# Hybrid decoder layer on one core: first norms, held-back sums and transfers moved in the paired projections

## The chip, the core and the metric

The kernel runs on one core of one Trainium2 chip. A core has five engines that run side by side: TensorE (PE in the profile; its weight loads are PEld) for matmuls, VectorE (DVE), ScalarE (ACT), GpSimd (POOL) and SyncE (SP), which here only issues DMAs. Each engine works through its own list of instructions in order. The engines wait for each other by semaphores. The metric is the time of one execution in device microseconds (us); lower is better.

## What is computed

One decoder layer on a sequence of 1024 tokens of width 1024, in float32:

```python
h = modulate(rms_norm(x), shift1, scale1)
proj = h @ w_in                      # 1024 x 3600, split into nine parts
# group A: 4 heads of gated linear attention (pairs P0, P1 in the kernel)
# group B: 4 heads of HGRN2 (H0, H1, H1, H1), forget = lb + (1-lb)*sigmoid(hf)
def chunk_gated_linear_attention(q, k, v, log_a, chunk=64):
    cum = cumsum(log_a within the chunk)
    q_rel, k_rel = q * exp(cum - cum_mid), k * exp(cum_mid - cum)
    scores = where(causal, q_rel @ k_rel.T, 0);  o_intra = scores @ v
    chunk_update = (k * exp(cum_last - cum)).T @ v
    state = exp(cum_last) * state + chunk_update      # scan over 16 chunks
    return o_intra + (q * exp(cum)) @ state_before
o = rms_norm(o, gain) * silu(gate)   # for each head, then concatenated
x = x + gate1 * (concat(o) @ w_out)
h = modulate(rms_norm(x), shift2, scale2)
x = x + gate2 * (square(relu(h @ w_mlp1)) @ w_mlp2)
return rms_norm(x, final_norm_g)
```

## The kernel before

Every matmul with weights is done in a split form. A float32 operand is written as a high part in the format fp32r and a low part, and a product is three matmuls: high times high, low times high, high times low. ACT copies the high part of a weight tile (`pw_hi`, `w_hi`, `wr_hi`), and POOL or DVE subtracts to get the low part (`pw_lo`, `w_lo`, `wr_lo`).

The stages follow each other on PE: transposes of x and norms; the groups P0, P1 and H0, in which each column block of `w_in` is a plain product with 2 x 8 x 3 matmuls; then, from about 225 us on, four "paired" groups (three H1 and the last, G); then the output projection (about 440 to 533 us) and the MLP.

In a paired group two pairs of column blocks are computed, the early one (p even) and the late one (p odd), eight pairs in all (p = 0 to 7). A pair is a 2 x 2 block product done by Strassen's scheme with seven smaller products: six (`pair_product`, P1 to P6, twelve 128x512 matmuls each, 4 tiles by 3) and a seventh, P7, which is cut in four pieces (`seventh_piece`, three matmuls each), whose input operand comes from HBM (`t3_scratch`, tiles `piece_x` for pieces 0 and 2, `piece_y` for 1 and 3). The sums of weight quarters that the scheme needs (`weight_sum_of`, kinds S1 to S4) and the sums of the results (`join`) are done by DVE. `copy_part` on ACT keeps a partial result. The sums of inputs for P5 and P4 (`t1`, `t4`, from `x_sum`) are made once, by DVE and ACT, before and in pair 0.

Between these products PE does the attention of the head before, in steps `attend(n)`: transposes (`k_end`, `vT`), chunk updates (`v_nat`, `k_nat`), scores (`q_rel`, `k_rel`), outputs (`masked`, `state`) and the sums of squares for the norm of a head ("ss", matmuls with `ones` on `sq_hi` and `sq_lo`). For the norm, ACT does a logarithm and an exponential (`norm_log`, `norm_exp`, in H0 inside `read_out`), each behind a load of another activation table, and DVE multiplies (`norms`).

The order on each engine is the order in which the code is written: nothing is scheduled by a planner. What an engine does late, all that stands behind it does late too. SP's list of DMAs is such a list as well: a `wait_ge` in it holds all later transfers back.

The names that matter below: on DVE, `group` ends H0, with `weight_sum_of(0, "S2")`, the sum and difference of `x_sum` (`add_parts`, `subtract`), the first norms (`read_out(7)`) and the gate; `paired` is a paired group (L2703 on). On ACT, `group` and `paired`; on PE, `two_pairs`; on SP, `load_piece`, `load_pair_quarter`, `load_out`, `load_x_back`.

## Time and profile before

| | us |
|---|---|
| median of 3 runs (lowest, highest) | 1165.41 (1165.19, 1165.82) |
| the profiled execution | 1166.44 |
| its span, first to last instruction | 1164.7 |
| PE busy | 1137.4 (98%) |
| DVE busy | 876.3 (75%) |
| ACT busy | 612.9 (53%) |
| POOL busy | 499.4 (43%) |
| mean granted clock of TensorE, share of full | 0.993 |

The busy time of PE counts each matmul from its start to its modelled end, and the next one starts before that end. So a gap on PE that is shorter than about 0.16 us doesn't show as idle, and one that shows is 0.16 us longer when counted from start to start. The times of the other engines are those of their instructions, waiting inside an instruction included. The DMA queues moved 180.44 MB, 155 GB/s on average.

### The profile page before, as it was taken

What the parts mean: (1) busy time and instruction counts of PE and PEld (TensorE: products, weight loads), DVE (VectorE), ACT (ScalarE), POOL (GpSimd) and SP (SyncE); (2) the same over time, 40 slices, a digit from 0 to 9 for tenths busy, and PEclk for the clock granted to TensorE, in tenths of its full rate; (3) what the DMA queues carried; (4) which work ended last, traced back from release to release, by engine and by line L of the source; (5) the groups of instructions that cost most, each with busy time, mean ns of one, the idle gap of its engine ahead of it and who ended that gap; (6) DMA issues with size and microseconds to landing.
All of it is one profiled execution on the core that took longest, in us unless ns stands there. A gap on an engine that the chain in (4) does not pass through costs nothing.

```text
span 1164.7 us, 15675 instructions
## 1 busy us (share of the span) xinstructions
PE 1137.4 (98%) x5555; PEld 939.3 (81%) x5555; DVE 876.3 (75%) x1048; ACT 612.9 (53%) x933; POOL 499.4 (43%) x318
## 2 busy tenths in 40 slices
PE   7999999899999999999999999999999999999996
PEld 6788788787878787888888888888888888788885
DVE  6898888877777677477976765677795884966776
ACT  7763564756566566345654555455664433424424
POOL 1021111534243344427534353344466675666741
PEclk9999999999999999999999999999999999999999
DMA  9777353044353549421455344544624637447203
GB/s 359 259 235 271 128 175 97 1 127 129 93 177 98 154 123 295 143 93 73 137 170 181 136 155 135 181 144 157 194 64 159 223 91 264 147 132 279 72 1 145
DMA packets 160549, 180.44 MB, mean 155 GB/s; under 512 B 7508, under 2 KB 119256, under 8 KB 157784
## 3 DMA queue, kind: packets, MB, share of 16 engines
q1 hardware_dynamic: 160472, 179.44, 46.4%
q8 instruction: 45, 0.74, 0.3%
q14 instruction: 32, 0.26, 0.1%
HBM read 138.51 MB, written 40.89 MB: 154 GB/s over the span
## 4 chain that ended last, share of the span: by engine, by line
PE 89%; DVE 4%; DMA 2%; ACT 2%; issue 1%; SPq 1%; POOL 1%; DVEq 0%; ACTq 0%
PE unit_bank L1742 16%; PE unit_bank L2156 9%; PE unit_bank L2158 9%; PE unit_bank L2157 9%; PE small_bank L2156 9%; PE small_bank L2158 9%; PE small_bank L2157 9%; PE unit_bank L2003 3%; PE small_bank L1742 3%; PE unit_bank L2005 3%; PE unit_bank L2004 3%; PE small_bank L1879 2%; DVE ada_acc L2257 1%; PE small_bank L1781 1%; DMA ada_slot<-in_w_ada_dram 1%
## 5 line engine op out<-in xcount | busy, mean ns | idle before, releaser
L997 POOL TENSOR_TENSOR wr_lo<-quarter,wr_hi 128x512 fp32r<-128x512 f32 x122 | 197.6, 1632 | 174.4 <-ACT wr_hi L1530 174.3
L2156 PE MATMUL unit_bank<-op_hi,wr_hi 128*128 128x512 f32 x452 | 176.5, 390 | 1.1 <-issue 1.1
L2158 PE MATMUL unit_bank<-op_hi,wr_lo 128*128 128x512 f32 x452 | 175.9, 389 | 0.0
L2157 PE MATMUL unit_bank<-op_lo,wr_hi 128*128 128x512 f32 x452 | 175.9, 389 | 0.0
L2156 PE MATMUL small_bank<-op_hi,wr_hi 128*128 128x512 f32 x448 | 174.5, 390 | 0.0
L2158 PE MATMUL small_bank<-op_hi,wr_lo 128*128 128x512 f32 x448 | 174.3, 389 | 0.0
L2157 PE MATMUL small_bank<-op_lo,wr_hi 128*128 128x512 f32 x448 | 174.3, 389 | 0.0
L1530 ACT ACTIVATE wr_hi<-wr_full 128x512 fp32r<-128x512 f32 x90 | 56.8, 631 | 173.3 <-DVE wr_full L2903 173.3
L2903 DVE TENSOR_TENSOR wr_full<-quarter,quarter 128x512 f32<-128x512 f32 x90 | 88.9, 989 | 56.3 <-PE small_bank L2158 23.0
L1530 ACT ACTIVATE wr_hi<-quarter 128x512 fp32r<-128x512 f32 x136 | 83.0, 626 | 90.5 <-PE unit_bank L2158 48.4
L1742 PE MATMUL unit_bank<-a_hi,w_hi 128*128 128x512 f32 x304 | 121.2, 399 | 0.8 <-DVE w_lo L2401 0.8
L1742 PE MATMUL unit_bank<-a_lo,w_hi 128*128 128x512 f32 x304 | 118.5, 390 | 0.0
L1742 PE MATMUL unit_bank<-a_hi,w_lo 128*128 128x512 f32 x304 | 118.4, 390 | 0.0
L997 POOL TENSOR_TENSOR wr_lo<-wr_full,wr_hi 128x512 fp32r<-128x512 f32 x48 | 80.2, 1673 | 77.0 <-ACT wr_hi L1530 65.6
L2156 PEld LDWEIGHTS unit_bank<-op_hi,wr_hi 128*128 128x128 f32 x452 | 84.8, 188 | 19.5 <-issue 2.1
L2157 PEld LDWEIGHTS unit_bank<-op_lo,wr_hi 128*128 128x128 f32 x452 | 84.9, 188 | 17.8 <-issue 0.2
L2158 PEld LDWEIGHTS unit_bank<-op_hi,wr_lo 128*128 128x128 f32 x452 | 84.8, 188 | 17.7
L2158 PEld LDWEIGHTS small_bank<-op_hi,wr_lo 128*128 128x128 f32 x448 | 84.1, 188 | 17.6
L2156 PEld LDWEIGHTS small_bank<-op_hi,wr_hi 128*128 128x128 f32 x448 | 84.1, 188 | 17.4 <-POOL wr_lo L997 0.2
L2157 PEld LDWEIGHTS small_bank<-op_lo,wr_hi 128*128 128x128 f32 x448 | 84.1, 188 | 17.4
L930 POOL TENSOR_TENSOR w_lo<-raw,w_hi 128x1024 fp32r<-128x1024 f32 x11 | 28.8, 2614 | 150.8 <-ACT w_hi L1054 150.8
L972 POOL TENSOR_TENSOR pw_lo<-pw_full,pw_hi 128x512 fp32r<-128x512 f32 x24 | 39.7, 1654 | 85.7 <-ACT pw_hi L1315 68.9
(366 smaller groups left out, 2397.2 us busy)
## 6 DMA issues: line engine op xcount, KB each, us to landing
quarter<-in_w_mlp_dram SPq DMA_DIRECT2D x128, 256.0 KB, 4.1
hidden_scratch<-hid SPq DMA_DIRECT2D x98, 256.0 KB, 2.4
ada_slot<-in_w_ada_dram SPq DMA_DIRECT2D x48, 512.0 KB, 6.1
op_full<-hidden_scratch SPq DMA_DIRECT2D x21, 1024.0 KB, 4.8
pair_quarter<-in_w_in_dram SPq DMA_DIRECT2D x32, 256.0 KB, 3.7
piece_x<-t_scratch SPq DMA_DIRECT2D x16, 512.0 KB, 4.1
piece_y<-t_scratch SPq DMA_DIRECT2D x32, 256.0 KB, 3.3
raw<-in_w_out_dram SPq DMA_DIRECT2D x16, 512.0 KB, 4.5
```

Source lines behind the costliest of these rows:

```text
L930: pool.tensor_tensor(w_lo[slot][:, :, :], raw[slot][:, :, :], w_hi[slot][:, :, :].bitcast(F32), ALU.subtract).then_inc(wlo_ready, 1)
L972: pool.tensor_tensor(pw_lo[place][:, :, :], pair_source(prod), pw_hi[place][:, :, :].bitcast(F32), ALU.subtract).then_inc(pair_lo, 1)
L997: pool.tensor_tensor(wr_lo[slot][:, :, :], split_source(n), wr_hi[slot][:, :, :].bitcast(F32), ALU.subtract).then_inc(wr_lo_pool, 1)
L1530: act.activation(wr_hi[slot][:, :, :], split_source(n), ACT.Copy).then_inc(wr_hi_ready, 1)
L1742: return pe.matmul(out_ap, left, right, start=start, stop=stop)
L2003: pe.matmul(dst, wh, hi[:, k, :], start=k == 0 and prod not in (P6, P3), stop=False, skip_group_check=True)
L2004: pe.matmul(dst, wh, lo[:, k, :], start=False, stop=False, skip_group_check=True)
L2005: mm = pe.matmul(dst, wl, hi[:, k, :], start=False, stop=k == KH - 1, skip_group_check=True)
L2156: pe.matmul(dst, wh, ah, start=opens, stop=False, skip_group_check=True)
L2157: pe.matmul(dst, wh, al, start=False, stop=False, skip_group_check=True)
L2158: mm = pe.matmul(dst, wl, ah, start=False, stop=k == KH - 1, skip_group_check=True)
L2903: dve.tensor_tensor(dst[:, :, :], a[:, :, :], b[:, :, :], op).then_inc(w_sum, 1)
```

## The change

The diff moves work; the arithmetic is the same. By part:

1. SP: a `piece_x` transfer of 512 KB becomes two of 256 KB. The copies of x back from HBM (`xT`, 4 x 1 MB) are no longer issued in one go ahead of the third weight tile of the output projection but one at a time between the weight tiles, and the eight first MLP quarters are issued after the eighth weight tile, not after the fourth.
2. ACT, end of H0: the two logarithms of the first norms stay, then come the copy of the keys and of the partial result and the high part of P6, then the two exponentials, the high part of P5 and the high part of `t4`.
3. DVE, same place: S2 of pair 0 is done before `decay` and `q_cum`; the sums of inputs for `t4` wait until the low part of P2 of pair 0 is made; S1 and the first join stand before the norms; the gate stands behind `t4_lo`.
4. PE, pair 0: pieces 1 and 2 of P7 stand behind P5, piece 3 behind P4. In all pairs: `attend(5)`, the first sum of squares, stands in the middle of P1 of the late pair.
5. All paired groups: ACT makes `sq_hi` before it copies the output; DVE does S4 and the second `sq_lo` of the late pair right after the first join, before `decay`, `q_cum` and `q_rel`; ACT does the high part of the next P7 before the second norm's logarithm and exponential, and the last value copy right behind them.

```diff
@@ SP
-                if j % 2:
-                    for i in range(2):
-                        sp.dma_start(piece_y[i][:, :].bitcast(F32), t3_dram[:, j, i, :]).then_inc(piece_y_loaded, 16)
-                else:
-                    sp.dma_start(piece_x[120 if p < 5 else 96][:, :, :].bitcast(F32), t3_dram[:, j]).then_inc(piece_x_loaded, 16)
+                for i, part in enumerate(piece_place(p, j)):
+                    sp.dma_start(part.bitcast(F32), t3_dram[:, j, i, :]).then_inc(piece_y_loaded if j % 2 else piece_x_loaded, 16)
...
-            for i in range(2):
-                load_x_back(i)
-            for v in range(2, 4):
+            load_x_back(0, 0)
+            load_out(2)
+            load_x_back(1, 0)
+            for v in range(3, OUT_HALVES):
                 load_out(v)
-            sp.wait_ge(normed, before("ss", 7))
...
+                if v in (5, 6):
+                    load_x_back(v - 5, 1)
+                if v == 7:
+                    sp.wait_ge(normed, before("ss", 7))
...
@@ ACT
-                    read_out(7, "ss")
-                    act.wait_ge(t_done, T_DONE_0 + 1)
...
-                    act.activation(tok(mixed[:, gi + 1], half), src, ACT.Copy).then_inc(read["o"], 1)
                     act.wait_ge(o_squared, before("o", gi) + half + 1)
                     act.activation(sq_hi[:, 0, :], stat[:, 0, :], ACT.Copy).then_inc(sq_hi_ready, 1)
+                    act.activation(tok(mixed[:, gi + 1], half), src, ACT.Copy).then_inc(read["o"], 1)
...
+                    first_logs()
+                    keys(0)
+                    copy_part(early, 0)
+                    pair_high(early, P6)
+                    first_exps()
+                    pair_high(early, P5)
+                    fourth_high()
                 pair_high(early, P4)
...
+                pair_high(late + 1, P7)
                 norm_log(1)
                 norm_exp(1)
-                pair_high(late + 1, P7)
+                value_of(0, late, "21")
                 pair_high(late + 1, P2)
-                value_of(0, late, "21")
@@ PE
+                    if between and k == 1:
+                        between()
...
                 pair_product(early, P6)
+                if early:
+                    seventh_piece(early, 2)
+                attend(2)
+                pair_product(early, P5)
                 if not early:
                     seventh_piece(early, 1)
-                seventh_piece(early, 2)
-                attend(2)
-                pair_product(early, P5)
-                seventh_piece(early, 3)
+                    seventh_piece(early, 2)
+                else:
+                    seventh_piece(early, 3)
                 attend(3)
                 pair_product(early, P4)
+                if not early:
+                    seventh_piece(early, 3)
                 attend(4)
                 pair_product(early, P3)
-                attend(5)
-                pair_product(late, P1)
+                pair_product(late, P1, lambda: attend(5))
@@ DVE
                 read_out(6)
+                if own == "H":
+                    weight_sum_of(0, "S2")
...
-                    weight_sum_of(0, "S2")
+                    dve.wait_ge(pair_lo, PAIR_LO_0 + split_of(0, P2))
                     add_parts(xs[2], 1, 0, 7)
                     subtract(xs[2], xs[2], xs[3], 8)
-                read_out(7)
+                if own == "P":
+                    read_out(7)
...
-                if own == "H":
-                    gate(u0 + 3, hh, hh)
...
                 join(early, "11")
+                if early == 0:
+                    first_norms()
                 states(0)
                 if early == 0:
                     low_fourth()
+                    first_gate()
...
                 join(late, "11")
+                weight_sum_of(late, "S4")
+                low_squares(1)
                 dve.wait_ge(read["up"], before("chunks", gi + 1))
...
-                weight_sum_of(late, "S4")
-                low_squares(1)
                 join(late, "u")
```

`first_logs`, `first_exps`, `first_norms`, `first_gate` and `fourth_high` hold the instructions that `read_out(7, "ss")`, `read_out(7)` and `gate` held before, with the same shapes.

DVE at the border of H0 and pair 0, before. `pair_quarter_186` is S2, `pw_full_201` S1, `pw_full_198` S4, `x_sum_204` the sum of inputs for `t4`, `unit_bank<-unit_bank,k_end` the first join, `COPY_PREDICATED` the mask of the first scores.

```order
L2584 COPY decay<-cum 128x16
L2587 SCALAR_TENSOR_TENSOR q_cum<-t_177,cum 128x1024
L2619 TENSOR_TENSOR pair_quarter_186<-pair_quarter_189,pw_full_199 128x512
L2408 TENSOR_TENSOR x_sum_204<-a_hi,a_lo 128x2048
L2414 TENSOR_TENSOR x_sum_204<-x_sum_204,x_sum_205 128x2048
L2493 SCALAR_TENSOR_TENSOR mixed<-mixed,cols,stat 128x512 x2
L2510 SCALAR_TENSOR_TENSOR t_177<-t_177,t_178 128x1024
L2515 SCALAR_TENSOR_TENSOR mixed<-t_177,mixed 128x1024
L2619 TENSOR_TENSOR pw_full_201<-pair_quarter_188,pair_quarter_189 128x512
L2646 TENSOR_TENSOR unit_bank<-unit_bank,k_end 128x512
L2679 SCALAR_TENSOR_TENSOR state<-state,decay,small_bank 128x128 x8
L2430 TENSOR_TENSOR t_lo<-x_sum_204,t_hi 128x2048
L2619 TENSOR_TENSOR pw_full_198<-pair_quarter_187,pair_quarter_186 128x512
```

And now:

```order
L2651 TENSOR_TENSOR pair_quarter_186<-pair_quarter_189,pw_full_199 128x512
L2600 COPY decay<-cum 128x16
L2603 SCALAR_TENSOR_TENSOR q_cum<-t_177,cum 128x1024
L2435 TENSOR_TENSOR x_sum_204<-a_hi,a_lo 128x2048
L2441 TENSOR_TENSOR x_sum_204<-x_sum_204,x_sum_205 128x2048
L2651 TENSOR_TENSOR pw_full_201<-pair_quarter_188,pair_quarter_189 128x512
L2678 TENSOR_TENSOR unit_bank<-unit_bank,k_end 128x512
L2621 SCALAR_TENSOR_TENSOR mixed<-mixed,cols,stat 128x512 x2
L2711 SCALAR_TENSOR_TENSOR state<-state,decay,small_bank 128x128 x8
L2457 TENSOR_TENSOR t_lo<-x_sum_204,t_hi 128x2048
L2628 SCALAR_TENSOR_TENSOR t_177<-t_177,t_178 128x1024
L2631 SCALAR_TENSOR_TENSOR mixed<-t_177,mixed 128x1024
L2651 TENSOR_TENSOR pw_full_198<-pair_quarter_187,pair_quarter_186 128x512
```

S2 went ahead of `decay`, S1 and the join ahead of the norms, and the two rows of the gate from before S1 to before S4.

PE in pair 0, before: the last matmuls of P6, pieces 1 and 2, the first scores, then P5 (`t_hi`).

```order
L2003 MATMUL unit_bank<-a_hi,pw_hi_190 128x512
L2004 MATMUL unit_bank<-a_lo,pw_hi_190 128x512
L2005 MATMUL unit_bank<-a_hi,pw_lo_194 128x512
L2023 MATMUL unit_bank<-piece_y_214,pw_hi_191 128x512
L2024 MATMUL unit_bank<-piece_y_215,pw_hi_191 128x512
L2025 MATMUL unit_bank<-piece_y_214,pw_lo_195 128x512
L2023 MATMUL unit_bank<-piece_x_212,pw_hi_191 128x512
L2024 MATMUL unit_bank<-piece_x_212,pw_hi_191 128x512
L2025 MATMUL unit_bank<-piece_x_212,pw_lo_195 128x512
L1742 MATMUL small_bank<-q_rel,k_rel 128x128 x4
L2003 MATMUL unit_bank<-t_hi,pw_hi_193 128x512
```

And now, behind P5: pieces 1 and 2, then the transposes of the second keys and the second scores, then P4.

```order
L2026 MATMUL unit_bank<-t_hi,pw_lo_197 128x512
L2046 MATMUL unit_bank<-piece_y_214,pw_hi_191 128x512
L2047 MATMUL unit_bank<-piece_y_215,pw_hi_191 128x512
L2048 MATMUL unit_bank<-piece_y_214,pw_lo_195 128x512
L2046 MATMUL unit_bank<-piece_x_212,pw_hi_191 128x512
L2047 MATMUL unit_bank<-piece_x_212,pw_hi_191 128x512
L2048 MATMUL unit_bank<-piece_x_212,pw_lo_195 128x512
L1802 MATMUL small_bank<-ident,k_end 128x128 x4
L1763 MATMUL small_bank<-q_rel,k_rel 128x128 x4
L2024 MATMUL unit_bank<-t_hi,pw_hi_192 128x512
```

The two pieces went behind the first scores and P5, so the second scores follow them closely; piece 3, which stood ahead of the key transposes, is now behind P4.

DVE in the late pair of a paired group (here p = 1), before: the first join, `decay`, `q_cum` (in `cum`), `q_rel`, S4 (`pw_full_198`), `sq_lo`, the second join.

```order
L2646 TENSOR_TENSOR unit_bank<-unit_bank,k_nat 128x512
L2755 COPY decay<-cum 128x16
L2760 SCALAR_TENSOR_TENSOR cum<-q_rel,cum 128x1024
L2763 SCALAR_TENSOR_TENSOR q_rel<-q_rel,t_177 128x1024
L2619 TENSOR_TENSOR pw_full_198<-pair_quarter_187,pair_quarter_186 128x512
L2686 TENSOR_TENSOR sq_lo<-stat,sq_hi 128x512
L2646 TENSOR_TENSOR t_178<-unit_bank,k_nat 128x512
```

And now:

```order
L2678 TENSOR_TENSOR unit_bank<-unit_bank,k_nat 128x512
L2651 TENSOR_TENSOR pw_full_198<-pair_quarter_187,pair_quarter_186 128x512
L2718 TENSOR_TENSOR sq_lo<-stat,sq_hi 128x512
L2792 COPY decay<-cum 128x16
L2797 SCALAR_TENSOR_TENSOR cum<-q_rel,cum 128x1024
L2800 SCALAR_TENSOR_TENSOR q_rel<-q_rel,t_177 128x1024
L2678 TENSOR_TENSOR t_178<-unit_bank,k_nat 128x512
```

S4 and `sq_lo` passed the three instructions that make `decay`, `q_cum` and `q_rel`.

## Rows read from the trace of the kernel before

**Rows 1.** The page, part 1: busy us (share of the span) and instructions.

```profile
PE 1137.4 (98%) x5555; PEld 939.3 (81%) x5555; DVE 876.3 (75%) x1048; ACT 612.9 (53%) x933; POOL 499.4 (43%) x318
```

**Rows 2.** Waits of PE, whole span: engine, line, waited for: us in total, times, longest.

```profile
PE small_bank L1742 <- DVE sq_lo L2686: 3.8, 6, 0.9
PE unit_bank L2003 <- POOL pw_lo L972: 1.9, 1, 1.9
...
PE unit_bank L2023 <- POOL pw_lo L972: 0.8, 1, 0.8
PE unit_bank L1742 <- DVE w_lo L2401: 0.8, 1, 0.8
PE small_bank L1781 <- ACT vT L1378: 0.3, 1, 0.3
```

**Rows 3.** Busy time by stretch: length, busy of PE, PEld, DVE, ACT, POOL, PEclk, DMA.

```profile
500.00:600.00 100.00, 100.00 (x439) 82.10 (x438) 86.72 (x86) 55.61 (x83) 49.83 (x32) 1.00 0.32 107
231.50:238.00 6.50, 6.02 (x18) 4.41 (x20) 5.61 (x6) 4.67 (x8) 2.49 (x2) 0.50 0.45 130
```

**Rows 4.** Timeline of PE, pair 0: start, us, instruction, count [idle before, releaser].

```profile
228.71 0.50 PE L2023 MATMUL unit_bank<-piece_x,pw_hi 128*128 128x512 f32 x1 [0.81 <-POOL pw_lo L972]
...
231.98 0.80 PE L2003 MATMUL unit_bank<-a_hi,pw_hi 128*128 128x512 f32 x1 [1.87 <-POOL pw_lo L972]
...
247.78 1.06 PE L1742 MATMUL small_bank<-q_rel,k_rel 128*128 128x128 f32 x8
...
254.01 0.48 PE L2003 MATMUL unit_bank<-a_hi,pw_hi 128*128 128x512 f32 x1
```

**Rows 5.** Timeline of POOL, pair 0 (us of each instruction).

```profile
225.40 3.26 POOL L972 TENSOR_TENSOR pw_lo<-pw_full,pw_hi 128x512 fp32r<-128x512 f32 x1 [2.73 <-DVE pair_quarter L2619]
228.62 3.31 POOL L972 TENSOR_TENSOR pw_lo<-pair_quarter,pw_hi 128x512 fp32r<-128x512 f32 x1
...
239.90 1.29 POOL L972 TENSOR_TENSOR pw_lo<-pair_quarter,pw_hi 128x512 fp32r<-128x512 f32 x1
```

**Rows 6.** Timeline of DVE, pair 0.

```profile
224.63 0.69 DVE L2619 TENSOR_TENSOR pair_quarter<-pair_quarter,pw_full 128x512 f32<-128x512 f32 x1
...
227.56 3.25 DVE L2414 TENSOR_TENSOR x_sum<-x_sum,x_sum 128x2048 f32<-128x2048 f32 x1
232.35 1.42 DVE L2493 SCALAR_TENSOR_TENSOR mixed<-mixed,cols,stat 128x512 f32<-128x512 f32 x2 [1.55 <-ACT stat L1234]
...
236.08 1.77 DVE L2619 TENSOR_TENSOR pw_full<-pair_quarter,pair_quarter 128x512 f32<-128x512 f32 x1
...
244.69 0.74 DVE L2666 COPY_PREDICATED masked<-causal,small_bank 128x512 f32<-128x512 uint32 x1
```

**Rows 7.** Timeline of ACT, pair 0.

```profile
230.40 1.28 ACT L1234 ACT_TABLE_LOAD   x1
231.69 1.15 ACT L1234 ACTIVATE stat<-stat 128x512 f32<-128x512 f32 x2
...
235.07 0.57 ACT L1329 ACTIVATE k_nat<-small_bank 128x512 f32<-128x512 f32 x1
```

**Rows 8.** Timelines of PE, DVE and ACT, end of pair 3 (late pair of the second paired group).

```profile
330.03 0.47 PE L1742 MATMUL small_bank<-sq_hi,ones 128*128 128x512 f32 x1 [0.95 <-DVE sq_lo L2686]
...
338.94 1.07 PE L1781 MATMUL small_bank<-ident,vT 128*128 128x128 f32 x8
...
325.07 2.27 DVE L2760 SCALAR_TENSOR_TENSOR q_cum<-q_rel,q_cum 128x1024 f32<-128x1024 f32 x1
...
332.51 0.68 DVE L2619 TENSOR_TENSOR pw_full<-pair_quarter,pair_quarter 128x512 f32<-128x512 f32 x1
...
338.22 0.58 ACT L1378 ACTIVATE vT<-unit_bank 128x512 f32<-128x512 f32 x1
```

**Rows 9.** Timelines of SP's queue and PE, first products of the output projection.

```profile
438.93 7.38 SPq L780 DMA_DIRECT2D raw<-in_w_out_dram  x2
...
452.46 0.50 PE L1742 MATMUL unit_bank<-a_hi,w_hi 128*128 128x512 f32 x1 [0.75 <-DVE w_lo L2401]
```

69 lines of the change are left out of this document (41 added, 28 removed).

## The prediction

> **What bounds the kernel now.** I read the page's shares first, then PE's waits, then busy time by stretch, then the timelines at each wait. The shares say that PE is busy 98% of the span, DVE 75%, ACT 53%, POOL 43% [rows 1]. PE runs the same 5555 matmuls after the change, so only its gaps and its clock can be won. The waits that the change aims at are few: six for the low part of the squares, 3.8 us, two for POOL's low parts, 1.9 and 0.8, one for the low part of an output weight, 0.8, and one for a value copy, 0.3 [rows 2]. Counted from start to start each is 0.16 longer, which makes about 4.8, 3.0, 0.9 and 0.5 us. One more loss is no wait: at 231.5 to 238.0 the granted clock is 0.50 of full, 1.2 GHz, and 18 matmuls took 6.02 us, against 439 in 100 us (0.228 each) at full clock [rows 3]. PE had just waited 0.81 at 228.71 and 1.87 at 231.98 [rows 4]. The 18 hold a few short ones, so I put the loss at 2.7 us rather than 6.02 - 18 x 0.228 = 1.9. All of it together is about 11.8 us, the most that can be won: 1165.4 - 11.8 = 1153.6.
>
> The sums below are made in the profiled execution, whose span is 1164.7 and whose own time is 1166.44, 1.03 above the median of 1165.41. The difference found there is taken off the median.
>
> **Output projection (part 1).** The third weight tile is issued at 438.93 and its transfer is followed by the wait of 0.75 for `w_lo` at 452.46 [rows 9], because 4 MB of `xT` stand ahead of it. Now 1 MB stands there. At the profile's mean of 155 GB/s 3 MB are some 19 us, at the rate of a busy stretch less, in each case far more than 0.75. The wait goes: -0.9. What was issued early is now late: the rest of `xT`, and 8 MLP quarters of 256 KB behind the eighth tile. They are needed at 533 us, after a stretch of 93 us in which PE is full; I cost them at 0, covered by that stretch, and at up to +1 if the last quarter is late for the first MLP product. Splitting `piece_x` in two costs SP another issue, 16 times, on a queue that runs ahead: 0.
>
> **End of H0 and pair 0 (parts 2 to 4).** Before, DVE does S2 at 224.63 and then, without a pause, the sum and the difference of `x_sum`; the difference took 3.25 against the 2.24 of the sum (from 225.32 to 227.56) [rows 6]. POOL's two low parts beside them took 3.26 and 3.31, and alone 1.29 [rows 5]. So the two engines exclude each other when both read two operands from SBUF, and each second one is 2 us late. Now S2 ends 0.9 earlier, at about 224.2, POOL starts earlier and alone, and P7's low part is there at about 226.5 and P2's at 227.8, instead of 228.66 and 231.93 [rows 5]. Both waits of [rows 4] and the low clock behind them go: 0.97 + 2.03 + 2.7 = 5.7.
>
> What is late next is DVE's own chain. The sums of inputs now wait for P2's low part, until 227.8; sum and difference then take 2 x 2.24, to 232.3, where before they ended at 227.56 + 3.25 = 230.81. From there to the first mask at 244.69 are 13.88 us, of which DVE waited 1.55 for the exponentials [rows 6], so 12.33 without that wait. The same instructions stand in that stretch after the change, in another order, with S1 (1.77) and a join first. (The 1.77 of S1 holds about 1.1 of standing behind POOL, against 0.69 for S2; POOL's low parts of P6 and P5 still lie beside this stretch, so I leave it in.) S1 and the join cover the wait: the exponentials, which come behind the key copy (0.57 [rows 7]), the high part of P6 and a load of 1.28, begin to land near 234.5 (the logarithms end at 230.4 plus the 0.65 that S2 puts ahead of `q_cum`, then 0.57 + 0.57 + 0.6 + 1.28 and half of 1.15). So the mask starts at 232.3 + 12.33 = 244.6, as before, and ends 0.74 later, at 245.35.
>
> The second scores go into the bank of the first and can't start before that. Before, PE reached them at 247.78 [rows 4], when the mask was long done. Now PE is there 5.7 earlier, less another 0.7 since piece 3 (three matmuls of 0.228) moved behind P4, plus a new wait: P6's high part is made behind the logarithms and the key copy, at about 232.6, and its low part, 1.29 later and behind the difference, at some 234.2, while PE comes to P6 at about 232.8. That is 1.4. So PE is at the second scores at 242.8 and waits 2.55. It goes on at 245.35 in place of 247.78 - 0.7: a lead of 1.7, and P3 starts at 252.3, not 254.01.
>
> Behind PE's second scores and `ss(0)` the next late thing is the turn to the next pair, where PE needs the value copy of ACT. That copy hangs on DVE's and ACT's chain (output, squares, norm, join, S3), which starts from a mask that is where it was. So of the lead of 1.7 most is returned there. I take -0.3 for the whole part; bounds: -1.7 if the chain has slack that I don't see, and +1.5 if it comes out later (the two waits that I add, 1.4 and 2.55, are to about 0.5 each).
>
> The Trainium skill, "ScalarE: Activation LUTs", section "What ACT_TABLE_LOAD costs", gives 1283 ns for the load and 1380 ns more of drain at each switch. The row has 1.28 at 230.40 and the exponential at 231.69, directly behind it [rows 7]: no second part shows after the load. By the page's price the exponentials would end 1.4 later, which is rival C; by the row they don't.
>
> **Late pairs (part 5, and `attend(5)` of part 4).** Before, PE waits for `sq_lo` twice a group, e.g. 0.95 at 330.03, since `sq_lo` stands behind `q_cum` (2.27) and more on DVE [rows 8]. With S4 and `sq_lo` ahead of them it is some 2 us earlier, and the wait goes; with the first `ss` in the middle of P1 the other goes as well. That is 1.6 a group, 4.8 in all. But the turn is tight already: the value copy runs 338.22 to 338.80 and PE's transposes start at 338.94 [rows 8]. It is ACT's, behind both table loads of the second norm, and these wait for S3 and the high and low parts of P7. On DVE, `q_cum` and `q_rel` are now some 1.4 later (S4 and `sq_lo` first), the second join 0.2 to 0.3 later, S3 at about 332.8 against 332.51. ACT wins something, because the high part of P7 and the logarithm are in a better order: I find the copy 0.3 earlier, at 337.95. So PE, ahead by 1.6, waits about 1.5 for it and keeps 0.3 a turn. There are three turns, of which the last two are sure: -0.6. Bounds: -4.8 if the copy moves with PE, +0.9 if it comes 0.3 later each time.
>
> **Sum.** -0.9 - 0.3 - 0.6 = -1.8: 1165.4 - 1.8 = 1163.6. From the bounds near it (part one -0.9 to 0, pair 0 -1 to +1, turns -1.5 to +0.9) the forecast's own range is 1162.2 to 1165.5.
>
> **Rivals.**
>
> A, the copy has slack: the waits for squares are truly saved and only pair 0 is given back. Then -0.9 - 0.3 - 4.8 = -6.0, 1159.4. For it: PE waited just 0.3 for a value copy in the whole span [rows 2], so it is a bottleneck once, not three times. Against it: 0.14 between the copy's end and PE's start at 338.94.
>
> A2, all is kept, pair 0 too: 1153.6. Against it: DVE's 12.33 us between difference and mask, which the change doesn't shorten.
>
> B, the other side: the new waits lower TensorE's clock. Before, 0.81 and 1.87 within 4 us put it at 0.50 for 6.5 us, at a cost of 2.7 [rows 3, 4]; single waits of 0.95 [rows 8] and 0.75 [rows 9] didn't. Now there are 1.4 at P6 and 2.55 at the second scores, and about 1.5 at three turns. In pair 0 a drop is paid from the lead. At the turns there is none: three drops would be 3 x 2.7 = 8.1, less the 1.8, or 1171.7; one or two of them 1166.3 to 1169.0. I take two, 1168 to 1169, as its time. It decides as soon as PE's wait at a turn, with what lies near it, weighs like the pair at 228.71 to 231.98.
>
> C, the exponentials are late. DVE comes to the norms at 232.3 + 1.77 + 0.7 = 234.8, only 0.3 behind their end by my count. If they end 1.4 later, the norms, the mask and all behind it come 1.1 later than before, and PE, which waits for that chain at the next turn, with them: -1.8 + 1.1 = -0.7, 1164.7. For it: ACT now does three operations more between the logarithms and the exponentials. Against it: the load of 1.28 has the exponential directly behind it [rows 7]. By the Trainium skill's price for a switch (same page and section) this is what would happen.
>
> D, the gain of part 1 is lost to a late MLP quarter (+1): 1164.6.
>
> **How the numbers follow.** Forecast 0.50 (in it that 0.02), A 0.27, A2 0.05, B 0.14, C and D 0.02 each. A measurement of this kernel tells 0.2%, 2.3 us, from no change. Faster than 1163.1 are A, A2 and about a fifth of the forecast: 0.42. Slower than 1167.7 is B, two drops or more, 0.12, and 0.02 for a turn that comes later than my bound. The rest, 0.44, is within. The range reaches over A to 1158.0 and on the other side to 1167.0, which leaves out A2 and most of B, 0.17.
>
> **What would show it.** Right: no wait for `w_lo` near 450; POOL's low parts of P7 and P2 in 1.3 each; DVE idle about 2.4 before the sum of inputs; the first mask at 244.6; PE waiting about 2.5 for it, and about 1.4 for P6's low part; the granted clock full around 231; waits for `sq_lo` under 0.5 in total beyond pair 0, and waits for the value copy up from 0.3 to 3 or 4 us. Wrong: a mask earlier than 243.5, a P3 of pair 0 and a turn both over 1 us earlier (A or A2), a clock of 0.50 behind a turn (B), norms on DVE after 235.5 (C), or a new wait at the start of the MLP (D).

## The result: slower by 0.6%

| | before | changed |
|---|---|---|
| median of 6 runs (lowest, highest) | 1166.41 us (1165.19, 1170.06) | 1174.27 us (1171.65, 1174.86) |
| span of the profiled execution | 1164.7 | 1172.1 |
| PE busy | 1137.4 | 1139.6 |

The ratio is 1.006, with a 95% interval of 1.0043 to 1.0077: slower, by 7 to 8 us, where 1.8 us less was forecast. The predicted range ended at 1167.0.

PE's waits in the profile of the changed kernel, which answer to [rows 2]; the columns are the same:

```profile
PE small_bank L1802 <- ACT vT L1391: 4.7, 3, 2.4
...
PE unit_bank L2046 <- POOL pw_lo L970: 2.3, 2, 1.2
PE unit_bank L2024 <- POOL pw_lo L970: 2.1, 3, 1.2
...
PE unit_bank L2024 <- DVE unit_bank L2678: 1.9, 3, 0.7
PE small_bank L1763 <- DVE masked L2698: 1.6, 1, 1.6
...
PE small_bank L1763 <- DVE sq_lo L2718: 1.0, 1, 1.0
```

The waits for `sq_lo` fell from 3.8 to 1.0 and those for `w_lo` are gone. In their place stand 4.7 for the value copy, 2.3 and 2.1 for POOL's low parts, 1.9 for a join, 1.6 for the mask. Where in the program this happens is best seen with PE's own landmarks: the first product of pair 0, the transposes of `vT` at the three turns from a paired group to the next, the first product with the third weight tile of the output projection, and the first product of the MLP. Both columns are differences of start times on PE's timeline.

| stretch of PE | before | changed | difference |
|---|---|---|---|
| to pair 0 | 224.91 | 224.72 | -0.19 |
| pair 0 to the first turn | 60.88 | 63.06 | +2.18 |
| first to second turn | 53.15 | 56.03 | +2.88 |
| second to third turn | 53.03 | 56.90 | +3.87 |
| third turn to the third weight tile | 60.49 | 60.50 | +0.01 |
| from there to the MLP | 77.25 | 77.07 | -0.18 |
| MLP to the end | 634.99 | 633.82 | -1.17 |
| sum, the span | 1164.7 | 1172.1 | +7.4 |

The loss is made between pair 0 and the third turn, +8.9 in all. PE's timeline there, changed kernel (start, us, instruction, idle before and its releaser):

```profile
234.00 0.50 PE L2024 MATMUL unit_bank<-a_hi,pw_hi 128*128 128x512 f32 x1 [1.21 <-POOL pw_lo L970]
...
241.89 0.50 PE L2046 MATMUL unit_bank<-piece_x,pw_hi 128*128 128x512 f32 x1 [0.55 <-DMA piece_x<-t_scratch]
...
244.83 2.08 PE L1763 MATMUL small_bank<-q_rel,k_rel 128*128 128x128 f32 x8 [1.55 <-DVE masked L2698]
...
287.78 1.06 PE L1802 MATMUL small_bank<-ident,vT 128*128 128x128 f32 x8 [1.13 <-ACT vT L1391]
290.00 0.47 PE L2046 MATMUL unit_bank<-piece_x,pw_hi 128*128 128x512 f32 x1 [1.15 <-POOL pw_lo L970]
...
335.65 0.47 PE L2024 MATMUL unit_bank<-a_hi,pw_hi 128*128 128x512 f32 x1 [0.65 <-DVE unit_bank L2678]
...
343.81 1.94 PE L1802 MATMUL small_bank<-ident,vT 128*128 128x128 f32 x8 [2.44 <-ACT vT L1391]
...
400.71 1.06 PE L1802 MATMUL small_bank<-ident,vT 128*128 128x128 f32 x8 [1.08 <-ACT vT L1391]
```

Pair 0 went as predicted up to the second scores: the two waits and the low clock at 231 are gone, PE waits 1.21 for P6's low part (1.4 forecast) and then, until 244.83, for the first mask, which DVE starts at 244.06 (244.6 forecast, 244.69 in [rows 6]). Of the two low parts that POOL now makes earlier, that of P2 took 1.29, as forecast, and that of P7 2.29, for 1.3 forecast. A wait of 0.55 for a `piece_x` transfer at 241.89 was not foreseen; it only shortens the wait for the mask. The turns did not go as predicted: at each PE waits 1.1 to 2.4 for the value copy, and the first piece of the next P7 starts 2.2 behind the transposes (at the first and third turn with a wait of 1.15 in between; at the second the transposes themselves are slow, 1.94 for 1.06). In the kernel before the piece started 1.18 behind them:

```profile
338.94 1.07 PE L1781 MATMUL small_bank<-ident,vT 128*128 128x128 f32 x8
340.12 0.47 PE L2023 MATMUL unit_bank<-piece_x,pw_hi 128*128 128x512 f32 x1
```

TensorE's granted clock falls at two places of this execution (busy time by stretch, columns as in [rows 3]):

```profile
245.00:250.00 5.00, 5.00 (x20) 4.39 (x21) 0.69 (x1) 0.99 (x2) 1.90 (x2) 0.71 0.72 229
345.00:350.00 5.00, 4.73 (x15) 3.58 (x14) 1.98 (x3) 3.21 (x7) 1.94 (x2) 0.50 0.22 65
```

At 345 to 350 that is the lower level, 1.2 GHz, throughout; at 245 to 250 it is a part at 1.2 and a part at 2.4 GHz. Now the chain that leads to the turn, on the engines that PE waits for. DVE of the changed kernel in the late pair ahead of the second turn:

```profile
326.83 0.69 DVE L2678 TENSOR_TENSOR unit_bank<-unit_bank,k_nat 128x512 f32<-128x512 f32 x1
327.43 1.19 DVE L2651 TENSOR_TENSOR pw_full<-pair_quarter,pair_quarter 128x512 f32<-128x512 f32 x1
328.58 1.73 DVE L2718 TENSOR_TENSOR sq_lo<-stat,sq_hi 128x512 fp32r<-128x512 f32 x1
330.24 1.26 DVE L2792 COPY decay<-q_cum 128x16 f32<-128x16 f32 x1
331.53 1.23 DVE L2797 SCALAR_TENSOR_TENSOR q_cum<-q_rel,q_cum 128x1024 f32<-128x1024 f32 x1
...
334.01 0.68 DVE L2678 TENSOR_TENSOR t<-unit_bank,k_nat 128x512 f32<-128x512 f32 x1
...
336.73 1.78 DVE L2651 TENSOR_TENSOR pw_full<-pair_quarter,pair_quarter 128x512 f32<-128x512 f32 x1
...
343.21 0.75 DVE L2725 SCALAR_TENSOR_TENSOR mixed<-mixed,cols,stat 128x512 f32<-128x512 f32 x1 [3.37 <-ACT stat L1363]
```

and POOL and ACT beside it:

```profile
328.02 1.75 POOL L970 TENSOR_TENSOR pw_lo<-pair_quarter,pw_hi 128x512 fp32r<-128x512 f32 x1
330.12 1.34 POOL L970 TENSOR_TENSOR pw_lo<-pw_full,pw_hi 128x512 fp32r<-128x512 f32 x1 [0.35 <-ACT pw_hi L1328]
336.45 1.51 POOL L970 TENSOR_TENSOR pw_lo<-pair_quarter,pw_hi 128x512 fp32r<-128x512 f32 x1 [4.98 <-ACT pw_hi L1328]
```

```profile
335.74 0.63 ACT L1328 ACTIVATE pw_hi<-pair_quarter 128x512 fp32r<-128x512 f32 x1 [1.01 <-DMA pair_quarter<-in_w_in_dram]
...
338.60 0.63 ACT L1328 ACTIVATE pw_hi<-pw_full 128x512 fp32r<-128x512 f32 x1 [1.74 <-DVE pw_full L2651]
339.25 1.28 ACT L1358 ACT_TABLE_LOAD   x1
...
341.26 1.28 ACT L1363 ACT_TABLE_LOAD   x1
342.55 0.63 ACT L1363 ACTIVATE stat<-stat 128x512 f32<-128x512 f32 x1
343.09 0.58 ACT L1391 ACTIVATE vT<-unit_bank 128x512 f32<-128x512 f32 x1
```

The same two joins and the end of the exponential in the kernel before:

```profile
323.77 0.69 DVE L2646 TENSOR_TENSOR unit_bank<-unit_bank,k_nat 128x512 f32<-128x512 f32 x1
...
329.80 0.68 DVE L2646 TENSOR_TENSOR t<-unit_bank,k_nat 128x512 f32<-128x512 f32 x1
```

```profile
336.64 0.63 ACT L1350 ACTIVATE stat<-stat 128x512 f32<-128x512 f32 x1
```

From join to join DVE took 6.03 us before and takes 7.18 now (326.83 to 334.01): S4, `sq_lo` and the small `decay` copy cost 1.19, 1.73 and 1.26, because POOL's low parts at 328.02 and 330.12 lie beside them. Start to start these three take 4.10, and took 1.90 before, where S4 and `sq_lo` needed 0.68 each. `q_cum` is quicker for it (1.23, [rows 8] has 2.27). Then S3 takes 1.78 beside POOL's 336.45, where it took 0.68 [rows 8]. From the join's start to the end of the exponential it was 7.47 us before (329.80 to 337.27) and is 9.17 now (334.01 to 343.18), because ACT's high part of P7 (338.60) waits for that S3 and the logarithm with its table load stands behind it. Together that is 1.15 + 1.70 = 2.85. From the end of the exponential to the first piece of P7 it is 2.85 in both kernels, and from that piece to the next first join 36.8 in both (36.80 and 36.83). So the 1.15 and the 1.70 are the whole loss of this period, counted from piece to piece: 53.15 before, 56.02 now (that the leg behind the exponential is 2.85 long as well is a coincidence). The value copy does come sooner behind the exponential (PE's transposes start 0.63 behind its end, before 1.67), but that wins nothing, because PE then stands at the piece.

The third period is made up otherwise. S3 took 0.69 at the third turn, so join to exponential is 8.08, 0.6 over the old 7.47; join to join is 7.18 again; and from the piece to the first join it is 38.80, 2.0 more than at full clock, in the stretch that begins with the low clock.

### The profile page after: what moved, and what is told of

Its sections match the earlier page's. It is cut to its first block, busy times and chain, and to the rows that moved or that the text cites. A ratio compares the mean times of both kernels' runs of the same rounds, so it can differ in the third digit from the quotient of the medians.

```text
span 1172.1 us, 15691 instructions
## 1 busy us (share of the span) xinstructions
PE 1139.6 (97%) x5555; PEld 940.7 (80%) x5555; DVE 877.7 (75%) x1048; ACT 612.9 (52%) x933; POOL 497.7 (42%) x318
## 4 chain that ended last, share of the span: by engine, by line
PE 82%; DVE 6%; ACT 4%; issue 3%; DMA 2%; POOL 1%; SPq 1%; DVEq 0%; ACTq 0%
PE unit_bank L1763 17%; PE unit_bank L2183 9%; PE unit_bank L2185 9%; PE unit_bank L2184 9%; PE small_bank L2185 9%; PE small_bank L2183 9%; PE small_bank L2184 9%; PE small_bank L1763 3%; PE unit_bank L2024 2%; PE unit_bank L2025 2%; PE unit_bank L2026 2%; DVE ada_acc L2284 1%; PE small_bank L1900 1%; PE small_bank L1802 1%; DMA ada_slot<-in_w_ada_dram 1%
## 5 line engine op out<-in xcount | busy, mean ns | idle before, releaser
L970 POOL TENSOR_TENSOR pw_lo<-pair_quarter,pw_hi 128x512 fp32r<-128x512 f32 x32 | 45.1, 1412 | 70.2 <-ACT pw_hi L1328 70.2
```

Source lines behind the costliest of these rows:

```text
L970: pool.tensor_tensor(pw_lo[place][:, :, :], pair_source(prod), pw_hi[place][:, :, :].bitcast(F32), ALU.subtract).then_inc(pair_lo, 1)
```

## The experiments

The landmarks of all kernels, in the same stretches; "ratio" is to the kernel before, of runs on the same chip, with its 95% interval.

| kernel | pair 0 to turn 1 | turn 1 to 2 | turn 2 to 3 | ratio |
|---|---|---|---|---|
| before | 60.88 | 53.15 | 53.03 | 1 |
| changed | 63.06 | 56.03 | 56.90 | 1.006 (1.0043 to 1.0077) |
| e1, late pairs undone | 64.10 | 53.70 | 53.61 | 1.0011 (0.9999 to 1.0023) |
| e2, ACT's turn undone | 61.77 | 53.92 | 54.36 | 1.0017 (1.0008 to 1.0025) |
| e3, DVE's turn undone | 60.78 | 54.14 | 54.06 | 1.0015 (1.0006 to 1.0024) |
| e4, attend(5) undone | 65.35 | 57.53 | 56.77 | 1.0093 (1.0077 to 1.0109) |
| e5, e1 with one `piece_x` | 60.77 | 53.21 | 52.99 | 1.0006 (0.9997 to 1.0015) |
| e6, ACT and DVE undone | 61.34 | 53.40 | 53.57 | 1.0004 (0.9996 to 1.0013) |
| e7, early logarithm | 60.58 | 52.73 | 52.73 | 0.9985 (0.9977 to 0.9994) |
| e8, e7 with one `piece_x` | 60.47 | 52.81 | 52.76 | 0.999 (0.9981 to 1.0) |
| e9, e8 with S4 back | 60.36 | 52.40 | 52.46 | 0.9985 (0.9976 to 0.9994) |
| e10, before with early logarithm | 59.31 | 52.70 | 52.70 | 0.9993 (0.9984 to 1.0002) |
| e11, join ahead of norms | 62.32 | 54.40 | 55.48 | 1.0049 (1.0035 to 1.0062) |
| e12, changed once more | 61.81 | 55.47 | 56.85 | one run |

The second period (turn 1 to 2) taken apart, counted from the first piece of one P7 to that of the next, in four legs: from that piece to the first of the two joins above, from there to the second join, from there to the end of ACT's exponential, from there to the next piece.

| kernel | piece to join | join to join | join to exponential | exponential to piece | sum |
|---|---|---|---|---|---|
| before | 36.80 | 6.03 | 7.47 | 2.85 | 53.15 |
| changed | 36.83 | 7.18 | 9.17 | 2.84 | 56.02 |
| e1 | 36.77 | 6.03 | 8.04 | 2.85 | 53.69 |
| e2 | 36.82 | 7.20 | 7.05 | 2.85 | 53.92 |
| e3 | 36.84 | 6.03 | 8.42 | 2.85 | 54.14 |
| e5 | 36.69 | 6.03 | 7.64 | 2.85 | 53.21 |
| e6 | 36.83 | 6.04 | 7.68 | 2.84 | 53.39 |
| e7 | 36.84 | 7.18 | 5.66 | 3.09 | 52.77 |
| e9 | 36.84 | 6.24 | 6.28 | 3.09 | 52.45 |
| e10 | 36.92 | 6.03 | 5.64 | 4.12 | 52.71 |
| e11 | 36.84 | 7.18 | 8.07 | 2.31 | 54.40 |

Where the last leg is 2.85 (2.31 in e11, which shortens it), the chain behind the exponential lets PE on. Where it is longer, PE is no longer held by it.

The theory (T): each turn is set by a chain over DVE and ACT, join, S3, high part of P7, logarithm, exponential, value copy, and the edits of the late pair lengthened it. The rival (R): what pair 0 gives back is the loss.

**e1.** The late pairs as before, SP and pair 0 changed:

```diff
-                pair_high(late + 1, P7)
                 norm_log(1)
                 norm_exp(1)
-                value_of(0, late, "21")
+                pair_high(late + 1, P7)
                 pair_high(late + 1, P2)
+                value_of(0, late, "21")
...
-                weight_sum_of(late, "S4")
-                low_squares(1)
...
-                pair_product(late, P1, lambda: attend(5))
+                attend(5)
+                pair_product(late, P1)
```

> The changed kernel with all edits of the late pairs and of the turn undone: S4 and the second sq_lo back behind q_rel, ACT's high part of P7 back behind norm_exp and the value copy back behind both high parts, sq_hi back behind the copy of the output, attend(5) back ahead of P1. SP's lists and pair 0 stay changed. Theory T (each turn is lengthened on the chain DVE join, S3, ACT high part of P7, logarithm, exponential, value copy): the two full periods from value transposes to value transposes go back from 56.0 and 56.9 us to 53.1, the clock stays full, and the kernel takes about as long as before, 0.999 to 1.001 of it. Rival R (what pair 0 gives back is what costs): the turns stay late, the ratio stays above 1.004.

Measured: 1.0011, periods 53.70 and 53.61. R falls: the turns come back with the late pair. But they come back only to 0.55 above the old ones, which is more than T allowed (53.1), and pair 0 to the first turn is the longest yet, 64.10, with waits of 1.25 for the mask and 2.31 for the first `sq_lo` and a low clock behind both. T had a full clock. The low one is seen in this one execution; the twelve runs spread from 1164.55 to 1170.72. The row of the third period that is late against before is on ACT (of e1 and of e5, the kernel below with one edit more):

```profile
390.53 0.63 ACT L1328 ACTIVATE pw_hi<-pair_quarter 128x512 fp32r<-128x512 f32 x1 [2.21 <-DMA pair_quarter<-in_w_in_dram]
```

```profile
385.01 0.64 ACT L1331 ACTIVATE pw_hi<-pair_quarter 128x512 fp32r<-128x512 f32 x1 [1.68 <-DMA pair_quarter<-in_w_in_dram]
```

ACT's high part of the next P1 waits for a weight quarter: 2.21 in e1, 1.68 in e5, 1.71 before. Both quarters are issued at the same place of the program; in e1 it lands 3.3 us after its issue, in the kernel before 2.8. `piece_x`, in two transfers, is issued just ahead of it.

**e2.** Only ACT's order at the turn undone (the first hunk of e1).

> The changed kernel with ACT's order at the turn as before (logarithm, exponential, high parts of P7 and P2, value copy). The logarithm no longer waits for S3 (1.74 us at 336.9) and POOL gets P2's high part before the value copy, so PE's wait of 1.15 for P7's low part goes. If ACT's order is the main cause, the period falls by 2 us or more a turn and the ratio to before is 1.001 or less. If DVE's order is (its second join 1.15 us later and S3 1.1 longer, both beside POOL's low parts), the period falls by about 1 and the ratio is 1.002 to 1.005.

**e3.** Only DVE's order undone (the second hunk of e1, with the two calls back behind `q_rel`).

> The changed kernel with S4 and the second sq_lo back behind q_rel on DVE. If DVE's order is the main cause: join to join on DVE goes from 7.2 back to about 6.0 us, S3 no longer meets POOL (0.68 for 1.78), the period falls by about 2 us a turn, at the price of PE's wait of 0.95 for sq_lo, and the ratio to before is 1.000 to 1.003. If ACT's order is, the period falls by less than 1 and the ratio is above 1.003.

Measured: 1.0017 and 1.0015, periods 53.92 and 54.36 (e2), 54.14 and 54.06 (e3). Each alone gives back 1.9 to 2.8 us a period, about what was written down for "the main cause" in both cases (the ratio of e2 is 0.0007 over the bound for it), so neither is "the" cause. The two don't add: with DVE's order alone left in (e2) a period is 0.5 and 0.8 over that with both undone (e6), with ACT's alone (e3) 0.7 and 0.5, with both 2.6 and 3.3 (the 3.3 holds the low clock of the third period). The table shows where it goes. In e2 the second join is 1.17 late, but ACT's high part of P1, behind which the logarithm stands, waits for a weight quarter in any case, and now waits 1.26 for it and not 2.27 as in e1: the lateness of the join disappears in that wait (7.05 for 8.04). In e3 S3 is on time, and the high part of P7 ahead of the logarithm costs about its own duration (8.42 for 8.04). Only with both does ACT wait for a late S3. With ACT's old order the logarithm starts although S3 isn't done:

```profile
336.11 1.82 DVE L2651 TENSOR_TENSOR pw_full<-pair_quarter,pair_quarter 128x512 f32<-128x512 f32 x1
...
336.51 1.28 ACT L1358 ACT_TABLE_LOAD   x1
```

The table load runs at 336.51 while S3 (336.11, 1.82 us) is still under way.

**e4.** Only attend(5) undone (the last hunk of e1).

> The changed kernel with attend(5), the first sum of squares of a pair, back ahead of P1 in place of its middle. Theory T gives it no part in the chain that ends at the value copy: periods within 0.3 us of those of the change, PE waits some 1.3 longer for the sq_lo of pair 0 and gains that at the next value copy; ratio to before as with the change, 1.005 to 1.007. A rival, that the norm's logarithm and what is behind it on ACT come later because ss is later on PE: the periods fall by 0.5 us or more.

Measured: 1.0093, slower than the change: periods 57.53 and 56.77, the wait for `sq_lo` in pair 0 2.29, and four stretches of low clock. S3 met POOL at two turns here (1.78 and 1.79), at one in the change. So the middle of P1 looks like the better place, though how much of the 1.0093 is low clock and how much the order isn't separated. My expectation of the same time was too good: the waits for `sq_lo` were expected to be regained at the value copy (2.46, 2.45 and 1.07 there; 1.13, 2.44 and 1.08 in the change) and were not.

**e5.** The kernel of e1 with `piece_x` in one transfer:

```diff
-                for i, part in enumerate(piece_place(p, j)):
-                    sp.dma_start(part.bitcast(F32), t3_dram[:, j, i, :])...
+                if j % 2:
+                    for i in range(2):
+                        sp.dma_start(piece_y[i][:, :].bitcast(F32), t3_dram[:, j, i, :])...
+                else:
+                    sp.dma_start(piece_x[...][:, :, :].bitcast(F32), t3_dram[:, j])...
```

> The kernel of e1_late_undone with piece_x brought in one transfer of 512 KB again. In e1 the periods from value transposes to value transposes were 53.70 and 53.61 us, not 53.15 and 53.03 as before, and the first row that is late is ACT's high part of P1, which waits for a pair_quarter that lands 3.3 us after its issue instead of 2.8. Theory (the two smaller transfers delay the weight quarter behind them, and that is on the chain to the value copy): the periods go back to 53.0 to 53.2. Rival (something else of pair 0 or of the order is carried on): they stay at 53.6.

Measured: 53.21 and 52.99, as theory has it. The split cost 0.5 to 0.6 us a period. Pair 0 to the first turn is 60.77 here, though PE waits 2.43 for the first `sq_lo`: the clock stays full. The ratio says something more. This kernel is parts 1 to 4 without the split and `attend(5)`, for which -0.9 and -0.3 were forecast, a ratio of 0.999; it measured 1.0006, with an interval that begins at 0.9997. The profiled execution, with 1164.54 the fastest of its twelve (median 1166.24), flatters it.

**e6.** ACT's and DVE's hunks undone together.

> The changed kernel with both ACT's order at the turn and S4 with the second sq_lo on DVE put back; attend(5) in the middle of P1 and sq_hi ahead of the output's copy stay. Each of the two alone brought the periods from 56.0 and 56.9 to about 54.1. If they lengthen the chain independently, both together give 53.6 (that of e1); if each alone was already hidden by PE's own waits, the periods stay at 53.9 to 54.2. Ratio to before 1.000 to 1.001.

Measured: 53.40 and 53.57, 1.0004, just under both forecasts. Together they give 0.5 to 0.8 more than either alone. What is left over 53.1 lies between join and exponential (7.68 for 7.47), where the split lay in e1; no run has this kernel with one `piece_x`, so that it is the split here too is not shown.

**e7.** The change, with ACT's order at the turn new:

```diff
                 tanh_of(t0, 0, late, "11")
+                norm_log(1)
                 pair_high(late + 1, P1)
                 act.wait_ge(filled["o"], before("o", gi + 1))
                 value_of(1, late, "22")
-                pair_high(late + 1, P7)
-                norm_log(1)
                 norm_exp(1)
-                value_of(0, late, "21")
+                pair_high(late + 1, P7)
                 pair_high(late + 1, P2)
+                value_of(0, late, "21")
```

> The changed kernel, with the second norm's logarithm on ACT moved ahead of the high part of the next P1, where ACT is idle 2 to 4 us, its exponential right behind the first value copy, and the high parts of P7 and P2 ahead of the second value copy. S4 and sq_lo stay early. Theory (what costs is only the chain logarithm, exponential, norms, join, tanh, gate to the next P7): the exponential ends 2.5 us earlier, PE's waits for the value copy and at the first piece of P7 fall under 0.3, periods 52.9 to 53.5, clock full at the turns, ratio 0.998 to 1.001. Rival (DVE's later joins cost by themselves): periods stay above 54.5, ratio above 1.003.

Measured: 0.9985, periods 52.73 and 52.73, no low clock. ACT at the second turn:

```profile
331.98 1.28 ACT L1358 ACT_TABLE_LOAD   x1
...
334.99 1.28 ACT L1363 ACT_TABLE_LOAD   x1
336.28 0.63 ACT L1363 ACTIVATE stat<-stat 128x512 f32<-128x512 f32 x1
...
337.86 0.58 ACT L1391 ACTIVATE vT<-unit_bank 128x512 f32<-128x512 f32 x1
```

The logarithm's load runs at 331.98, in the time in which ACT waited for the weight quarter. DVE's order is that of the change, its joins are as late as there (7.18 us from 324.07 to 331.25), and it costs little once the two tables aren't behind it (e9 gives the amount): PE's waits at the turn are 0.20 and none, its wait for the join stays at 0.65. The ratio's interval lies below 1. The rival of this run falls.

**e8.** e7 with `piece_x` in one transfer (the hunk of e5).

> As e7_log_early, with piece_x in one transfer. If the weight quarter that lands later is still on the chain, the periods are 0.3 to 0.6 us shorter than in e7; if the early logarithm hides it, they are equal. Ratio 0.997 to 1.000.

Measured: 52.81 and 52.76, equal to e7: with the logarithm ahead of P1's high part the quarter that lands 0.5 later is waited for by nobody.

**e9.** e8 with S4 alone back behind `q_rel`:

```diff
-                weight_sum_of(late, "S4")
                 low_squares(1)
...
+                weight_sum_of(late, "S4")
                 join(late, "u")
```

> The kernel of e8_log_early_one with S4 alone back behind q_rel on DVE; the second sq_lo stays early. In the changed kernel S4 took 1.19, sq_lo 1.71 and decay 1.26 us beside POOL's low parts, where alone each takes 0.68, and the join behind them came 1.15 later. If the order that puts them beside POOL is the cause, one of these collisions goes, the join comes 0.5 or more earlier, PE's wait of 0.65 for it falls under 0.3, and the periods fall from 52.8 to 52.3 to 52.6. If the whole collision stays with sq_lo, the periods stay at 52.7 to 52.9. Ratio 0.997 to 0.999.

Measured: 52.40 and 52.46, the wait of 0.65 down to 0.30, and the join 6.24 us after the one before (323.50 to 329.74). DVE:

```profile
325.25 1.28 DVE L2721 TENSOR_TENSOR sq_lo<-stat,sq_hi 128x512 fp32r<-128x512 f32 x1 [1.07 <-ACT sq_hi L1356]
326.46 0.17 DVE L2794 COPY decay<-q_cum 128x16 f32<-128x16 f32 x1
```

`decay` takes 0.17 us in place of 1.26 and `sq_lo` 1.28 in place of 1.73: two of the three collisions are gone or smaller, and S4, now behind `q_rel`, takes 0.69. With 0.9985 it is the fastest with e7; between these two the comparison can't tell.

**e10.** The kernel before with the early logarithm alone (`norm_log(1)` moved up as in e7, nothing else).

> The kernel before with one edit on ACT: the second norm's logarithm ahead of the high part of the next P1, the exponential where the logarithm stood. Theory: there the chain to the value copy was just behind PE (a wait of 0.28 at the first turn, none at the others), so the edit gains under 0.5 us a turn: periods 52.9 to 53.2, ratio 0.998 to 1.000. It would show that the early logarithm pays only together with the early sq_lo. Rival (each turn was bound by that chain all along): periods 52.5 or less, ratio 0.998 or less.

Measured: 52.70 and 52.70, 0.9993. The periods fell by 0.45 and 0.33, to between what the theory (52.9 to 53.2) and what the rival (52.5 or less) had. The first piece of P7 now stands 0.79 behind the transposes, before 1.18: 0.4 us a turn were lost there, too short for the profile to show as idle, so the kernel before was bound by this chain at its turns too. The expectation that the early logarithm pays only together with the early `sq_lo` did not hold: the periods are those of e7 (52.73), without any edit of the late pair on DVE and PE. The ratio can't be told from 1, nor from that of e7, whose interval it overlaps.

**e11.** The change with two calls on DVE exchanged:

```diff
-                norms(1)
                 join(late, "12")
+                norms(1)
```

> The changed kernel with join(late, 12) ahead of norms(1) on DVE. Theory: the first piece of the next P7 waits for exponential, norms, join, tanh, gate, not for POOL's low part that the profile names; without the norms ahead of the join, ACT's tanh is bound by its own queue and comes 0.3 to 0.4 us earlier, and PE's wait of 1.15 at the piece falls to 0.7 to 0.9; periods 0.3 to 0.4 shorter, ratio 1.004 to 1.006. Rival (POOL's low part is what it waits for): the wait stays 1.15 and the periods are as with the change.

Measured: the wait at the piece fell from 1.15 to 0.62 and the periods to 54.40 and 55.48, by 1.6 and 1.4. The direction is that of the theory, the size is not: 0.53 of it is the piece (2.31 for 2.84 from the exponential on). The other 1.1 of the 1.6 comes from S3, which takes 0.68 at this turn (at 336.22) and 1.78 in the change: a start that is 0.5 earlier misses POOL, and PE's wait for the value copy is 1.08 for 2.44. In the third period it is the other way round: here S3 meets POOL (1.78 at 390.61, +1.1), and the change had its low clock (-2.0, 36.83 for 38.80); with the 0.53 that makes the 1.4. How the profile names the wait is the lesson: in the change the piece at 290.00 is put down to POOL, whose low part ended at 289.50, and these rows of DVE and ACT end right before it:

```profile
287.18 0.75 DVE L2725 SCALAR_TENSOR_TENSOR mixed<-mixed,cols,stat 128x512 f32<-128x512 f32 x1 [2.18 <-ACT stat L1363]
287.85 0.69 DVE L2678 TENSOR_TENSOR unit_bank<-unit_bank,k_nat 128x512 f32<-128x512 f32 x1
289.21 0.69 DVE L2684 SCALAR_TENSOR_TENSOR t<-t,unit_bank 128x512 f32<-128x512 f32 x1 [0.66 <-ACT t L1381]
```

```profile
288.58 0.60 ACT L1381 ACTIVATE t<-unit_bank 128x512 f32<-128x512 f32 x1 [0.42 <-DVE unit_bank L2678]
```

Norms, join, ACT's tanh (288.58 to 289.18), gate (289.21 to 289.90), PE at 290.00. So T has the chain right up to the exponential, but what holds PE at its end is this piece, not the value copy.

**e12.** The changed kernel again, one execution.

> The changed kernel once more, for its profile alone: are the two stretches at a granted clock of about half, behind the second scores of pair 0 (244.8) and behind the value transposes of the second turn (343.8), a property of the program? If the waits ahead of them decide it, both stand at the same places and the periods are again 56.0 and 56.9 us. If it is chance from one execution to the next, one of them is gone or stands at another turn, and the period next to it is about 2.8 us shorter; the waits of 1.1 to 2.4 for the value copy stay in either case.

Measured: the low clock behind the second scores is gone (ahead of it PE waited 1.72, more than the 1.55 of the first execution), that behind the second turn is there again (0.67 of full in 345 to 350). Pair 0 to the first turn is 61.81 for 63.06. So the first is chance from one execution to the next, the second came in both. What POOL meets on DVE changes too: ahead of the second turn it is now `k_end` (2.32 for 1.22), `q_rel` (2.12 for 1.23) and the gate (1.45 for 0.69), and `sq_lo` and `decay` take 0.68 and 0.16. The exponential ends late all the same, and the period is 55.47.

## Why the prediction was wrong, step by step

**What bounds the kernel: half right.** PE's gaps that the profile shows were counted rightly, and that the value copy is "tight already" was seen. What was missed is that at a turn a second chain runs beside it, exponential, norms, join, tanh, gate, first piece of P7, which needs the same exponential and holds PE longer. It ends 2.85 behind the exponential in the kernel before and in the change, and in e10, where PE is free of it, a period is 0.4 shorter.

**Output projection: right.** The wait for `w_lo` is gone, and the MLP isn't late (PE is busy 93.00 of the 93 us from 440 to 533). In the change the 0.91 was used up in the same stretch by a wait of 1.15 at the piece behind the third turn; in e1 and e2, without that wait, the stretch is 59.61 and 59.42, for 60.49. Rival D, a late MLP quarter, falls with it. The -1.17 behind the start of the MLP I don't count as the change's: e10, with SP's list of before, shows -0.8 there.

**Splitting `piece_x` "on a queue that runs ahead: 0": wrong.** It cost 0.55 a period where the chain was tight (e1 against e5) and nothing where it wasn't (e7 against e8). In the kernel before ACT waits 1.7 at that place for the quarter, which the prediction did not look up.

**End of H0 and pair 0: the waits right, the gain not shown.** Forecast -0.3 to the first turn. With the late pairs undone it is -0.1 (e5, one execution). The -0.3 and -0.4 of e7 and e8 can't be read so, since the early logarithm shortens the first turn as well: the kernel before with that edit alone (e10) is at 59.31, quicker than any kernel with the new pair 0 (60.36 to 60.58 with the early logarithm). Up to the late pair's first join, ahead of any edit of the turn, it is 45.47 before, 44.31 in e10 (the same code up to there, with a granted clock of 0.74 and not 0.50 in 231.5 to 238.0), and 45.6 to 46.0 with the new pair 0 at full clock (e5, e7, e8, e9, e12). So what the two old waits and their low clock cost (5.7 by the forecast) is given back at the new waits, as forecast, and a little more with it. The price that was not in the sum is the clock: in the changed kernel's profile PE lost about 1.2 us behind the mask, by 63.06 against 61.81 in e12.

**Late pairs, "-0.6": here the prediction failed.** "The copy 0.3 earlier" became 2.9 later. Three terms: `q_rel` was put 1.4 later, but S4, `sq_lo` and `decay` met POOL's low parts and took 2.2 more than before, less 1.0 that `q_cum` won, and the join came 1.15 later, not 0.2 to 0.3. S3 met POOL as well, 1.1 more, at the second turn (at the other two it took 0.68 and 0.69). And "ACT wins something, because the high part of P7 and the logarithm are in a better order" was the wrong way round: the high part of P7 depends on S3, the logarithm doesn't, and two table loads were put behind that wait. The value copy, moved right behind the exponential, did win 1.0 there, and PE lost it again at the piece. The bound of +0.9 for all turns was too small by 6: the two full periods alone came to +6.75, of which about 2.0 are low clock.

**The forecast's own range.** The bounds that it is said to come from add up to -3.4 and +1.9, 1162.0 to 1167.3, and not to 1162.2 to 1165.5. The measured time lies outside of both.

**Rival B: the place and the sign, partly.** The low clock is there, at one turn in each of two executions and once in pair 0. Its price at the turn: the third period begins with it, and from the first piece of P7 to the first join PE and DVE need 38.80 for 36.83, so 2.0 us. B forecast 2.7 for a drop. But B held the clock for the loss, and it is the smaller part (about 2.0 at the turn and 1.2 in pair 0, of 7.4); the lengthened chain gives +2.9 in a period at full clock. Rivals A and A2 fall; C's norms came on time in pair 0 (234.29, for 234.8 forecast).

**The rule on table loads.** A row of the change agrees with the rows of before: a load at 339.25 for 1.28 and the logarithm at 340.55, the next load at 341.26, which takes 1.28 too, and the exponential at 342.55. The Trainium skill's 1.38 us of drain beside the 1.28 ("ScalarE: Activation LUTs", "What ACT_TABLE_LOAD costs") shows in no idle time here.

**The rule on the shared port.** POOL's low part and DVE's two-operand sums exclude each other: S4 and S3 took 1.19 to 1.82 beside one, for 0.68. The Trainium skill ("SBUF — State Buffer", "SBUF: two separate sides") says that whichever of the two starts first holds the lock for its whole instruction and the other stands, and that a DVE operation takes it in a two-port mode, or with two SBUF inputs against a GpSimd operation that reads SBUF. The trace agrees, and even a copy of 128x16 elements stood 1.1 us: 1.26 against 0.17 (e9). The prediction used this in pair 0 and left it out in the late pair.

## What to carry to other kernels

Before an instruction is moved ahead on an in-order engine, ask which of its inputs is the latest, and what independent work now stands behind that wait; here it was a logarithm, an exponential and their two table loads. Before a sum is moved on DVE, look at what GpSimd does in the stretch that it moves into, not at its duration where it was. And when two chains end at the same point (value copy and gate), taking a wait out ahead of them only moves it: shorten what both share, here the logarithm and exponential, by putting them into a time in which the engine waits for something else.

## What the runs showed that I had not expected

The same wait need not lower the clock. At the first `sq_lo` of pair 0 PE waited 2.43 us with full clock behind it (e5), 2.31 and 2.29 with half the clock behind (e1, e4). At the first mask it waited 1.55 with a drop and, in the same program, 1.72 without (changed, e12), and 2.35 without in e3. What decides it stays open. An issue of two smaller transfers ahead of a third made that one land 0.5 us later, at the same issue time. The best kernel found is e7 (or e9, which can't be told from it), 0.9985 of the kernel before. But e10, the kernel before with the early logarithm alone, has 0.9993 and an interval that overlaps theirs: beyond that one edit no part of the change is shown to win time.
